# Sixteen experts written out, their rest slots gathered four experts at a time

## What is computed

```python
N_EXPERTS, TOP_K_EXPERTS, D_MODEL, D_EXPERT = 16, 2, 1024, 256

def moe(x, w_router, b_router, w_gate, w_up, w_down):
    ...
    gate = ...                      # (tokens, experts), two of 16 not zero for a token
    out = jnp.zeros((B * T, D), F32)
    for e in range(N_EXPERTS):
        h = jax.nn.silu(xf @ w_gate[e]) * (xf @ w_up[e])
        out = out + gate[:, e:e + 1] * (h @ w_down[e]).astype(F32)
    return out.reshape(B, T, D).astype(x.dtype)

x = layer_norm(ALPHA * x + moe(x, ...), ln2_g, ln2_b)
```

## Time and profile before

| | |
|---|---|
| median of 3 runs | 1520.9 us (1512.1 to 1523.42) |
| the profiled execution's span | 1520.2 us |
| TensorE busy | 1318.4 us, 87% of the span |
| first gate product to the last down product of the experts | 1114.6 to 1439.5 us |
| mean granted TensorE clock, whole span | 0.880 |

### The profile page before, as it was taken

One profiled execution on the slowest core, in us unless ns is written; L12 is line 12 of the kernel. 1 busy time (PEld: TensorE's weight loads), 2 busy tenths in 40 slices (PEclk: granted clock), 3 DMA queues, 4 the chain that ended last, 5 costly groups with the idle time before them and its releaser, 6 DMA issues. The chain is left out here.

```text
span 1520.2 us, 16147 instructions
## 1 busy us (share of the span) xinstructions
PE 1318.4 (87%) x5597; PEld 813.6 (54%) x5597; DVE 775.7 (51%) x1787; ACT 398.4 (26%) x805; POOL 431.7 (28%) x460
## 2 busy tenths in 40 slices
PE   5898899999999999999898997996289999999800
PEld 2566565755656656656654544653156666666500
DVE  0024125778778878988897988333300000000078
ACT  1142424324324224224314212311011111111111
POOL 5103024052151251261055012002231111113487
PEclk9999899999999898999898988575679999999955
DMA  8966645536543443443333333001078766667163
GB/s 272 313 200 210 231 145 179 173 108 201 155 159 123 146 147 112 146 147 108 113 113 122 110 94 118 1 14 29 4 252 301 235 218 234 211 203 250 35 221 121
DMA packets 146265, 238.60 MB, mean 157 GB/s; under 512 B 17211, under 2 KB 117474, under 8 KB 146194
## 3 DMA queue, kind: packets, MB, share of 16 engines
q1 hardware_dynamic: 131298, 197.66, 40.3%
q0 software_dynamic: 10064, 29.16, 5.9%
q10 hardware_dynamic: 4832, 10.88, 2.3%
HBM read 211.38 MB, written 26.29 MB: 156 GB/s over the span
## 5 line engine op out<-in xcount | busy, mean ns | idle before, releaser
L1188 PE MATMUL bank_pair<-win,xT 128*128 128x384 f32 (+7 forms) x1152 | 450.6, 542 | 14.8 <-DMA win<-in_w_in 13.7
L1188 PEld LDWEIGHTS bank_pair<-win,xT 128*128 128x128 f32 (+1 forms) x1152 | 213.3, 193 | 192.0 <-issue 100.9
L897 DVE MAX8 top<-score 128x8 f32<-128x384 f32 (+6 forms) x201 | 174.9, 870 | 4.0
L898 DVE MATCH_REPLACE8 score<-top,score 128x384 f32<-128x384 f32 (+6 forms) x201 | 171.9, 855 | 0.0
L1282 PE MATMUL bank_pair<-w_out,yT 128*128 128x512 f32 (+1 forms) x288 | 131.2, 610 | 0.4 <-ACT yT L623 0.4
L1641 DVE COPY rows<-bank_pair 32x1024 f32<-32x1024 f32 x16 | 19.4, 1212 | 170.3 <-PE bank_pair L1677 170.3
L567 POOL TENSOR_TENSOR small<-small,pexp 128x4 f32<-128x4 f32 (+1 forms) x9 | 9.4, 1049 | 335.9 <-DVE small L1078 335.9
L1677 PE MATMUL bank_pair<-wd,hT 128*128 128x512 f32 (+1 forms) x192 | 98.8, 653 | 0.0
L1551 POOL DMA_INDIRECT xg<-x_rows,ids x32 | 30.1, 941 | 229.1 <-PE bank_pair L1656 215.9
L1282 PEld LDWEIGHTS bank_pair<-w_out,yT 128*128 128x128 f32 (+1 forms) x288 | 52.8, 186 | 74.0 <-issue 72.2
L1142 PE MATMUL bank_pair<-ident,lm 128*128 128x128 f32 (+2 forms) x234 | 43.2, 312 | 45.8 <-ACT lm L733 15.8
(11 more groups left out here) (339 smaller groups left out, 2091.7 us busy)
## 6 DMA issues: line engine op xcount, KB each, us to landing
win<-in_w_in SPq DMA_DIRECT2D x90, 768.0 KB, 4.4
win<-in_w_in SPq DMA_DIRECT2D x18, 1024.0 KB, 5.3
win<-in_w_in SPq DMA_DIRECT2D x18, 840.0 KB, 5.2
win<-in_w_in SPq DMA_DIRECT2D x18, 800.0 KB, 4.6
wg<-in_w_exp_gate SPq DMA_DIRECT2D x12, 1024.0 KB, 6.2
wu<-in_w_exp_up SPq DMA_DIRECT2D x12, 1024.0 KB, 9.4
wd<-in_w_exp_down SPq DMA_DIRECT2D x12, 1024.0 KB, 11.1
expert_rows<-rows ACTq DMA_DIRECT2D x16, 512.0 KB, 3.3
```

The costliest lines, as they stand in the source:

```text
L897: step(V.max(top8[0:n], sc))
L898: step(V.match_replace(sc, top8[0:n], sc, NEG))
L1188: last = mmul(zb[0:n, 0:w], xT[:, kk, 0:n], win[:, i % NWIN, k, 0:w], start=(kk == 0), stop=(kk == KD - 1))
```

## The change

The loops over experts are gone: all 16 are written out, so that semaphore counts are constants. The token ids of all experts are loaded at the start by SyncE, in one transfer for the 128 slots of every expert and 16 for the 32 rest slots, four experts' rests to a column of 128. GpSimd gathers the rests of four experts with one indirect transfer into `xgr`; TensorE turns them together in front of the turn of the first of the four, ScalarE copies them to `xrT`, and VectorE copies an expert's 32 columns per chunk from there into `xgT` (`rest_columns`). The turn of an expert is 8 transposes of 128 rows, four per bank. The down product of the 128 slots runs first, in one piece; then that of the 32 slots, in four matmuls of 256 columns per half `f`, each into another group of 32 columns of the array and so into another 32 partitions of `OB`, which has two buffers now. VectorE copies it as 128 x 256, and ScalarE stores it with four transfers.

```diff
-        ids = sb("ids", [128, NW, 2], I32)
-        xg = [sb(f"xg{j}", [128, 2, D]) for j in range(2)]
+        G4 = 4
+        NGR = NE // G4
+        ids = sb("ids", [128, NE + NGR], I32)
+        xg = [sb(f"xg{j}", [128, 1, D]) for j in range(2)]
+        xgr = sb("xgr", [128, D])
+        xrT = sb("xrT", [128, KD, 128])
...
+        def turns_before(e):
+            return 2 * e + 2 * (e // G4 + 1)
...
             def _(sp):
...
+                    sp.dma_start(ids[:, 0:NE], slots_e[0:128, :, 0]).then_inc(S("ids_loaded"), 16)
+                    for g in range(NGR):
+                        for j in range(G4):
+                            sp.dma_start(ids[CB * j:CB * j + CB, NE + g:NE + g + 1], slots_e[128:CAP, G4 * g + j:G4 * g + j + 1, 0]).then_inc(
+                                S("ids_rest_loaded"), 16)
+                sp.wait_ge(S("xg_loaded1"), 16)
+                for e in range(1, NE):
+                    if e >= NW:
+                        sp.wait_ge(S("ob_ps"), e - NW + 1)
                     for w, src in ((wg, "gate"), (wu, "up"), (wd, "down")):
+                        sp.dma_start(w[e % NW], wsrc[src][:, e]).then_inc(S(f"w_loaded{e % NW}"), 16)
...
             def _(pool):
+                pool.wait_ge(S("ids_loaded"), 16)
+                for e in range(NE):
+                    if e % G4 == 0:
+                        g = e // G4
+                        if g == 0:
+                            pool.wait_ge(S("ids_rest_loaded"), 16 * NE)
+                        else:
+                            pool.wait_ge(S("xgT_ps"), turns_before(G4 * (g - 1)))
+                        pool.indirect_dma_start(out=xgr[:], out_offset=None, in_=x1_d,
...
+                    if e >= 2:
+                        pool.wait_ge(S("xgT_ps"), turns_before(e - 2) + 2)
+                    pool.indirect_dma_start(out=xg[e % 2][:, 0, :], out_offset=None, in_=x1_d,
...
             def _(act):
+                def turned(e):
+                    u = turns_before(e)
+                    if e % G4 == 0:
+                        if e:
+                            act.wait_ge(S("rest_copied"), e)
+                        for q in range(2):
+                            act.wait_ge(S("xgT_ps"), u - 2 + q + 1)
+                            A.activation(xrT[:, 4 * q:4 * q + 4, :], T[q].rearrange("p (k n) -> p k n", k=4), ACT.Copy).then_inc(S("xgT_copied"), 1)
+                    for q in range(2):
+                        act.wait_ge(S("xgT_ps"), u + q + 1)
+                        A.activation(xgT[:, e % 2, 4 * q:4 * q + 4, 0:128], T[q].rearrange("p (k n) -> p k n", k=4), ACT.Copy).then_inc(S("xgT_copied"), 1)
...
+                    act.wait_ge(S("ob_copied"), e + 1)
+                    for j in range(G4):
+                        act.dma_start(rows_e[128:CAP, e, 256 * j:256 * j + 256], rest[e % 2][CB * j:CB * j + CB, :]).then_inc(S(f"rest_stored{e % 2}"), 16)
...
             def _(dve):
+                def rest_columns(e):
+                    dve.wait_ge(S("xgT_copied"), turns_before(G4 * (e // G4)))
+                    j = e % G4
+                    V.tensor_copy(xgT[:, e % 2, :, 128:CAP], xrT[:, :, CB * j:CB * j + CB]).then_inc(S("rest_copied"), 1)
...
+                    V.tensor_copy(rest[e % 2][:], OB[e % 2][:, 0:D // G4]).then_inc(S("ob_copied"), 1)
...
             def _(pe):
-                    for u in range(4):
-                        pe.wait_ge(S("xgT_copied"), e * 4 + (u + 1))
-                        for k in (2 * u, 2 * u + 1):
-                            c = CAP * (k % 2)
-                            E.transpose(T[u % 2][:, c:c + 128], xg[j % 2][:, 0, 128 * k:128 * k + 128], ident[:])
-                            last = E.transpose(T[u % 2][:, c + 128:c + CAP], xg[j % 2][0:CB, 1, 128 * k:128 * k + 128], ident[0:CB, 0:CB])
+                def turn(src, first):
+                    for q in range(2):
+                        if first + q >= 2:
+                            pe.wait_ge(S("xgT_copied"), first + q - 1)
+                        for k in range(4):
+                            c = 128 * (4 * q + k)
+                            last = E.transpose(T[q][:, 128 * k:128 * k + 128], src[:, c:c + 128], ident[:])
                         last.then_inc(S("xgT_ps"), 1)
...
+                    for f in range(2):
+                        pe.wait_ge(S("h_ready"), 2 * e + f + 1)
+                        for c in range(2):
+                            last = E.matmul(OA[:, 512 * c:512 * c + 512], hT[:, f, 0:128], wd[j][:, f, 512 * c:512 * c + 512],
+                                            start=(f == 0), stop=(f == 1))
+                    last.then_inc(S("oa_ps"), 1)
+                    if e >= 2:
+                        pe.wait_ge(S("ob_copied"), e - 1)
+                    for f in range(2):
+                        for c in range(G4):
+                            last = E.matmul(OB[e % 2][CB * c:CB * c + CB, 0:256], hT[:, f, 128:CAP], wd[j][:, f, 256 * c:256 * c + 256],
+                                            start=(f == 0), stop=(f == 1))
+                    last.then_inc(S("ob_ps"), 1)
```

More of the change, by code:

```diff
@@ L1494, in mlps @@
         hT = sb("hT", [128, 2, CAP])
-        rows = [sb(f"rows{j}", [128, 2, D]) for j in range(2)]
+        rows = [sb(f"rows{j}", [128, 1, D]) for j in range(2)]
+        rest = [sb(f"rest{j}", [128, D // G4]) for j in range(2)]
         most = sb("most", [128, NE])
@@ L1506, in mlps, with loaded @@
         more_e = em_d.rearrange("(e s) d -> s e d", e=NE)
[L1512 to L1518, removed]
+        def turns_before(e):
+            return 2 * e + 2 * (e // G4 + 1)
+        def loaded(e):
+            return 48 * (e // NW + (1 if e % NW else 0))
         with nc.Block() as block:
@@ L1522, in _ @@
             def _(sp):
[L1523 to L1527, removed]
-                    for w, src in ((wg, "gate"), (wu, "up"), (wd, "down")):
[L1529 to L1535, removed]
+                with nc.allow_non_contiguous_dma("slot ids"):
+                    sp.dma_start(ids[:, 0:NE], slots_e[0:128, :, 0]).then_inc(S("ids_loaded"), 16)
[3 more added lines that the diff above has]
+                                S("ids_rest_loaded"), 16)
@@ L1579, in body @@
[L1579 to L1592, removed]
@@ L1645, in _ @@
                 E = nc.tensor
[L1646 removed]
+                E.matmul(OB[1][:, 0:NE], ones[:], chosen_sum[:], start=True, stop=True).then_inc(S("counts_ps"), 1)
                 pe.wait_ge(S("most_ready"), 2)
[L1649 to L1657 removed]
@@ new lines, in turns @@
+                def turns(e):
+                    if e % G4 == 0:
+                        pe.wait_ge(S("xgr_loaded"), 16 * (e // G4 + 1))
+                        turn(xgr, turns_before(e) - 2)
+                    pe.wait_ge(S(f"xg_loaded{e % 2}"), 16 * (e // 2 + 1))
+                    turn(xg[e % 2][:, 0, :], turns_before(e))
+                turns(0)
+                for e in range(NE):
+                    j = e % NW
+                    if e:
+                        pe.wait_ge(S(f"w_loaded{j}"), loaded(e))
+                    pe.wait_ge(S("xgT_copied"), turns_before(e) + 2)
+                    pe.wait_ge(S("rest_copied"), e + 1)
```

110 lines of the change are left out of this document (44 added, 66 removed).

## The result

The changed kernel takes 1421.75 us (median; 1418.59 to 1429.01) against 1516.5 us for the kernel before in the same series: a ratio of 0.9387, with a 95% interval from 0.9345 to 0.9428. That is 94.8 us less where 80.5 were forecast. Times are compared between fast runs; of the first copy of the changed kernel further down, one run of four (1441.19 us) is a slow one and is left out of its median.

The account below looks back on a forecast made before the run. TensorE's instruction stream in the experts' stage was taken as the bound. Loop 240.7 us against 324.9 (-84.2), start +3.0, end +0.7: 1520.2 - 80.5 = 1439.7, forecast 1440 us, range 1428 to 1464.

Parts of the forecast that it names:

- What bounds the kernel: Experts' stage, 325.5 us of the 1520.2 us span: TensorE's instruction stream sets its length; other engines wait for TensorE.
- The 32-slot half, four at a time: Down product: 16 matmuls of 256 columns run four at a time in column groups, 1.1 us instead of 3.66; chance 0.58.
- The rivals of two groups: 32-slot half of the down product: only two of four groups run at once, 1.9 us, kernel 1453 us; chance 0.17.
- no overlap: 32-slot half of the down product: groups run one at a time, 3.6 us, kernel 1480 us; chance 0.08.
- The turn, 1.2 us: Transposes of an expert's tokens: 12 turns of 1.2 us and 3 of 2.8, 22.8 us in place of 51.2.
- The 128-slot half, 3.63 us: Down product of the 128 slots in one piece: four matmuls in 1.92 us, four more at 0.43, 3.63 us.
- The lower clock: Loop: six stretched down products go, 9 us; rival, three long turns keep the low clock, 1444 us, chance 0.03.
- The start, +3.0 us: Before the first gate product: id loads delay expert 0's gather 5.3 us, shorter turn; 3 us late, bounds 1 and 8.
- The end and ScalarE, +0.7 us: Last expert: four store issues, shorter copy, +0.7 us; ScalarE stays covered; GpSimd's residual rows covered by 5 us.
- that other side: ScalarE's stores: down product held up from 2.1 us per small store, over 1% slower from 3.6; case's chance 0.04.
- The DMA rival: Expert loop: DMA queues, 89% busy, become the bound; an expert takes 16 us, kernel 1456 us; chance 0.10.
- The base: Whole kernel: the sum starts from the profiled 1520.2 us, taken as good as the runs' median of 1520.9.

## Why the prediction was right and where it was off

*What bounds the kernel.* Right: the stage was TensorE's stream. The loop shrank by 91.4 us, what came off that stream: turns 15 x 3.41 - (12 x 0.87 + 3 x 2.34) = 33.7; down products 16 x (7.50 - 4.53) = 47.5; seven low-clock stretches of 1.4 to 1.7 us, some 11; less 1.1 us for a slower first product. Their sum is 91.1. The runs that undo the parts agree: 40.8 for the overlap, 39.4 for the turn with three of the stretches, some 6 for the other four, and 16 x 0.32 = 5.1 for the halves in one piece, together 91.3.

*The 32-slot half, four at a time.* Right, by one step further than the row behind it showed: two groups were read from the earlier trace rows, four were extrapolated. 1.00 us against 1.1. Of the 0.2 us "to begin and switch" about half was there: four sets of four matmuls at 0.22, and 0.1 us more around them. The rivals of two groups (1453 us) and of no overlap (1480) are refuted for this kernel, and the runs that force them show what they would have been: the half at 1.84 and 3.55 us, as the sums of 1.9 and 3.6 had it, and times of 1436 and 1460, 17 and 20 below the rivals' figures, as the forecast itself lay 18 above the time.

*The turn, 1.2 us.* Mis-sized: 0.87, so 4.0 us too much over twelve. What was too much are the 0.2 us for a late first transpose and the 0.1 us for a change to the down product. The late first transpose of the earlier trace rows stands in front of a 32-row one; with one shape throughout nothing is late, and eight follow each other at 0.109. The long turn, 2.8, was 2.34: the wait for the copy is there, but once (0.40 us), not long enough to hold both halves; 1.4 us over three.

*The 128-slot half, 3.63 us.* 3.53; 1.6 us over sixteen. The figure was built on four matmuls that began behind a change of shape. The run with the old turn shows that the 0.1 us belongs to that change: there it is 3.63 again. Running the halves in one piece each is worth 7.50 - (3.63 + 3.55) = 0.32 us per expert, with the 3.63 behind the old turn and the 3.55 of the run in one group; the prediction's 3.63 and 3.6 held 0.27 of it.

*The lower clock.* Right that it would go with the short turns, and that the three long ones might keep it didn't come true: the loop has none. Six stretches on the down products were counted, the trace of before has seven.

*The start, +3.0 us.* 4.7. The issue of the small loads (0.50 us each against 0.45) and the first gather's delay were near, 5.9 us against 5.3. What was off is the turn: 5.6 us from the first transpose to the first gate product, where 4.7 were taken from 5.8 of before. The first gate and up product, which counts to the loop, then took 11.64 us against 10.51, at a granted clock of 0.76 against 0.85.

*The end and ScalarE, +0.7 us.* +1.0: four issues of 2.13 us in all at the last expert. Within the loop the price of a store was mis-sized: 0.4 us each was taken, the median is 0.53, one took 2.27, and the longest set of four 4.14 us, on average 1.0 each. That is half of the 2.1 at which ScalarE would have held up the down product, and TensorE never waits for hT, so that other side did not come; it was nearer than 0.4 made it look. The slack of 5 us for GpSimd came out at 5.01.

*The DMA rival.* Not met: no wait for a transfer in the loop. The estimate of 89% busy was close to the 0.87 of the loop and the 0.94 of its middle.

*The base.* This is the step that failed and put the time outside the range. The sum starts from one profile of before, 1520.2 us, and holds its trunk and combine to be the same in the changed kernel: they stand in it at nothing, without a reason. The time came out 18.2 us below the forecast. The terms that the sum did have make 5 of these: 7 us too little in the loop's gain, 2 us too little in the losses at start and end, which alone would have given 1434.5 us, inside the range. Another 3.7 are the base, since before had a median of 1516.5 us in the series of the result. The last 9 lie in the trunk and the combine: -9.9 and -1.5 us in the two profiles, and some 8 us for the trunk in the means of all runs. The range had bounds for every term but none for these, though the runs of before that were known spread by 11 us.

One slip in the sum went unpunished: the loop's 240.7 us are a sum of pieces, set against the measured 324.9, while the same pieces of before make 322.4. Like against like the gain would have been 81.7. The 2.5 us between hold the seventh stretch of the lower clock, which stood behind the first expert's turn and did go.

## What to carry to other kernels

Matmuls with at most 32 output rows are worth dealing to different column groups of the array, and matmuls and transposes of one shape worth running in one piece: the first gave 40.8 us here, the short turns 39.4 with their stretches of the lower clock. A long run of transposes alone has cost more than its own time here, by the clock behind it; with the shorter one both went. And where single stages are summed to a total, the stages that nobody touched need a width of their own, taken from how far runs of the same kernel lie apart; and before a difference in such a stage is called chance, the means of many runs of both kernels should be compared.

## What the runs showed of the hardware

- Four column groups of 32 run side by side with little loss: four fp32 matmuls of 256 columns in 0.42 us, where one takes 0.38, and the same product in 1.00 us, where one group needs 3.55.
- Transposes of one shape follow each other every 0.11 us; a pair of a 128-row and a 32-row one takes 0.43. If a 32-row one alone costs no more than a 128-row one, which no run shows, half of the pair's price, 0.21 us, comes with the alternation. A matmul behind it begins 0.1 us late.
- The same program's trunk of 1.1 ms ended at 1099.1 us in one execution and at 1090.3 in another, while the loop behind it was 324.8 us in both. A difference of over half a per cent in a whole time can come from a stage that the edit doesn't reach.
- The issue of a small load costs SyncE 0.50 us when 16 stand in a row, 0.65 when four with four ids per row do, and that of a store of 32 rows costs ScalarE 0.31 to 2.27 us; dropping twelve of them brought the first gather 5.1 us nearer.
